# Log decays of each SSD head fetched from DRAM over all partitions instead of spread by TensorE, and the first four heads' exponentials one half earlier on ScalarE

## What is computed

```
acs = jnp.cumsum(dtc * a.reshape(g, r), axis=2)
acs_t = jnp.moveaxis(acs, 2, -1)
seg = acs_t[..., :, None] - acs_t[..., None, :]
decay_in = jnp.exp(jnp.where(lower, seg, -jnp.inf))
cb = jnp.einsum('bcign,bcjgn->bcgij', cc, bc)
xdt = xc * dtc[..., None]
y_diag = jnp.einsum('bcgij,bcgrij,bcjgrp->bcigrp', cb, decay_in, xdt)
```

## Time and profile before

| | us |
|---|---|
| median of 3 runs (2890.13 to 2893.3) | 2892.05 |
| the profiled execution | 2892.8 |
| its span, first to last instruction | 2890.1 |
| PE busy | 2823.3 (98%) |
| DVE busy | 1770.8 (61%) |
| ACT busy | 1498.3 (52%) |
| share of the DMA queue of SP (q1) in 16 engines | 55.5% |

### The profile page before, as it was taken

How to read it: one execution, slowest core, us unless ns; L and a number is a source line. 1 busy time by engine, 2 the same in 40 slices (tenths; PEclk the granted TensorE clock), 3 DMA queues, 4 the chain that set the end, 5 groups by cost and what they waited for, 6 DMA issues and landing times.

```text
span 2890.1 us, 41967 instructions
## 1 busy us (share of the span) xinstructions
PE 2823.3 (98%) x17088; PEld 2398.9 (83%) x17088; DVE 1770.8 (61%) x2255; ACT 1498.3 (52%) x2226; POOL 219.4 (8%) x275
## 2 busy tenths in 40 slices
PE   7999999999999999999989999999999999999997
PEld 4888998888777898877669889988887888897886
DVE  2487888886444555544455878888864444554555
ACT  3356776774333445533334567767743434544443
POOL 0001111120000000000110011111200000000000
PEclk9999999999999999999999999999999999999999
DMA  9944445545777644567896454455457565554664
GB/s 392 339 159 161 159 163 170 181 153 197 279 273 290 207 159 151 172 244 274 285 345 180 161 167 154 164 175 178 155 194 287 196 201 172 161 175 153 204 219 174
DMA packets 166849, 594.28 MB, mean 206 GB/s; under 512 B 20500, under 2 KB 22804, under 8 KB 166272
## 3 DMA queue, kind: packets, MB, share of 16 engines
q1 hardware_dynamic: 155376, 558.24, 55.5%
q0 software_dynamic: 11216, 33.34, 4.1%
q10 hardware_dynamic: 64, 0.02, 0.0%
HBM read 577.85 MB, written 13.66 MB: 205 GB/s over the span
## 4 chain that ended last, share of the span: by engine, by line
PE 86%; DMA 6%; DVE 5%; ACT 1%; issue 1%; SPq 0%; DVEq 0%; POOLq 0%; POOL 0%; ACTq 0%
PE PM L413 18%; PE PM L425 17%; PE PM L414 17%; PE PM L429 7%; PE PM L418 7%; PE PM L419 7%; PE A L638 5%; DMA raw<-in_w_in 2%; PE A L450 2%; DMA raw<-in_w_out 2%; DMA Zt<-in_w_mod 2%; DVE w_l L391 2%; PE A L635 1%; DVE X L1422 1%; DVE arena L1382 1%; PE PM L635 1%
## 5 line engine op out<-in xcount | busy, mean ns | idle before, releaser
L391 DVE TENSOR_TENSOR w_l<-raw,w_h 128x1024 fp32r<-128x1024 f32 (+1 forms) x880 | 1058.2, 1213 | 986.1 <-ACT w_h L386 977.3
L386 ACT ACTIVATE w_h<-raw 128x1024 fp32r<-128x1024 f32 (+1 forms) x880 | 905.4, 1046 | 827.5 <-PE PM L425 304.7
L413 PE MATMUL PM<-w_h,hT_h 128*128 128x512 f32 x1408 | 565.2, 401 | 2.1 <-issue 2.1
L414 PE MATMUL PM<-w_h,hT_l 128*128 128x512 f32 x1408 | 550.0, 391 | 0.0
L418 PE MATMUL PM<-hT_h,w_h 128*128 128x256 f32 x1920 | 485.6, 291 | 4.8 <-ACT w_h L386 2.5
L419 PE MATMUL PM<-hT_l,w_h 128*128 128x256 f32 x1920 | 469.7, 282 | 0.0
L413 PE MATMUL PM<-w_h,Z 128*128 128x512 f32 x1024 | 405.4, 396 | 9.5 <-ACT w_h L386 5.8
L414 PE MATMUL PM<-w_h,Z 128*128 128x512 f32 x1024 | 399.5, 390 | 0.0
L418 PEld LDWEIGHTS PM<-hT_h,w_h 128*128 128x128 f32 x1920 | 366.5, 191 | 16.2 <-issue 7.2
L425 PE MATMUL PM<-w_l,hT_h 128*128 128x512 f32 x1408 | 377.7, 390 | 0.7 <-DVE w_l L391 0.7
L419 PEld LDWEIGHTS PM<-hT_l,w_h 128*128 128x128 f32 x1920 | 367.1, 191 | 6.6 <-issue 4.8
(11 more groups left out here) (191 smaller groups left out, 2272.7 us busy)
## 6 DMA issues: line engine op xcount, KB each, us to landing
raw<-in_w_in SPq DMA_DIRECT2D x608, 512.0 KB, 4.2
raw<-in_w_ps SPq DMA_DIRECT2D x128, 512.0 KB, 5.3
raw<-in_w_mod SPq DMA_DIRECT2D x112, 512.0 KB, 4.3
Zt<-in_w_mod SPq DMA_DIRECT2D x80, 512.0 KB, 14.1
raw<-in_w_pa SPq DMA_DIRECT2D x64, 512.0 KB, 4.4
raw<-in_w_out SPq DMA_DIRECT2D x64, 512.0 KB, 6.0
arena<-in_state_ssm_fwd POOLq DMA_DIRECT2D x16, 256.0 KB, 3.8
arena<-in_state_ssm_bwd POOLq DMA_DIRECT2D x16, 256.0 KB, 3.7
```

The lines of the kernel that those rows point to most:

```text
L386: act.activation(w_h[:, k % RING, :, 0:n], half_raw(k, n), ACT.Copy).then_inc(hi_ready, 1)
L391: dve.tensor_tensor(w_l[:, k % RING, :, 0:n], half_raw(k, n), w_h[:, k % RING, :, 0:n].bitcast(F32), ALU.subtract).then_inc(lo_ready, 1)
L413: pe.matmul(tok_out(s), hi[:, kt, tk], wh, start=kt == 0, stop=False, skip_group_check=True)
L414: pe.matmul(tok_out(s), lo[:, kt, tk], wh, start=False, stop=False, skip_group_check=True)
```

## The change

The 64 x 512 table of log decays is written once per layer to a DRAM scratch tensor `h_dram`, by ACT's queue. SP then copies a head's row of 2 KB into all 128 partitions of `E[h % 4]` (256 KB), 128 times in all. ACT's `Relu` reads and writes `E` in place. PE's `decay` matmul, `sel` and `H` are gone, and the transposed running sums are computed in one copy of 64 rows instead of two. `exp` of heads 0 to 3 stands one half earlier (behind halves 1 to 4), that of heads 4 to 7 stands where it was (behind halves 6 to 9). `squares` writes its unused squares to `zs` instead of `E[0]`.

```diff
 LOAD_OF_HALF, LOAD_OF_TILE = raw_order()
+def decay_loads():
+    after = {}
+    for layer in range(DEPTH):
+        for q in range(NG):
+            body = 8 * layer * CHUNKS + 8 * (PH_SSD + 2 * (q + 1))
+            for h, at in enumerate((-1, 0, 5, 6, 11, 12, 13, 14)):
+                after[body + at] = (layer, q, h)
+    return after
+DECAY_LOADS = decay_loads()
 HOLDS = dict([(n, ("half", i)) for i, n in enumerate(LOAD_OF_HALF)] + [(n, ("tile", i)) for i, n in LOAD_OF_TILE.items()])
...
                 sp.dma_start(Zt[:, z_slot(m), :], mod_words(m)).then_inc(z_loaded[z_slot(m)], DMA)
+            def decay_row(L, q, h):
+                G = L * NG + q
+                if q == 0 and h == 0:
+                    sp.wait_ge(s_("H_stored"), (L + 1) * DMA)
+                if h >= 4:
+                    sp.wait_ge(s_("y_part"), G * HG + h - 3)
+                elif h >= 2:
+                    sp.wait_ge(s_("stT_done"), G + 1)
+                elif G:
+                    sp.wait_ge(s_("y_part"), (G - 1) * HG + 5 + h)
+                row = h_dram[L, q * HG + h:q * HG + h + 1, :].to_broadcast([P, 4 * P])
+                sp.dma_start(E[h % 4].rearrange("p d s n -> p (d s n)"), row).then_inc(e_loaded[h % 4], DMA)
             def half(L, c, i, w, block):
...
                     tile_to_z(m)
+                if k in DECAY_LOADS:
+                    decay_row(*DECAY_LOADS[k])
             def chunk(L, c, w, block, halves=8):
...
                     pe.wait_ge(s_("chw_ready"), L + 1)
-                    pe.wait_ge(s_("const_cast"), 1)
                     fp32(A[:, 3, 0:256].rearrange("p (d s n) -> p d s n", d=2, s=2)[:, 0], Umat, SA[:, 8:10, :], True)
...
                     for ds in range(4):
-                        for w in range(2):
-                            mm = fp32(A[NH * w:NH * w + NH, 0, ds * P:(ds + 1) * P], SA[:, 8 + ds, :], (Umat, Lmat)[ds // 2], ds == 0)
+                        mm = fp32(A[0:NH, 0, ds * P:(ds + 1) * P], SA[:, 8 + ds, :], (Umat, Lmat)[ds // 2], ds == 0)
                     mm.then_inc(s_("acsT_done"), 1)
...
                     mm.then_inc(s_("stT_done"), 1)
-                def decay(q, h):
-                    if h == 0:
-                        pe.wait_ge(s_("H_ready"), L + 1)
-                        pe.wait_ge(s_("ST_ready"), L * NG + q + 1)
-                    if h >= 2:
-                        pe.wait_ge(s_("exp_done"), (L * NG + q) * HG + h - 1)
-                    b = A[:, 2 + h % 2, :]
-                    mm = pe.matmul(b, sel[:, q * HG + h:q * HG + h + 1].to_broadcast([P, P]), H[:].rearrange("p d s n -> p (d s n)"),
-                                   start=True, stop=True, skip_group_check=True)
-                    mm.then_inc(s_("decay_done"), 1)
                 def y_start(q):
...
                     for h in range(HG):
-                        st[h] = [lambda h=h: decay(q, h)] + st.get(h, [])
                         st[4 + h] = st.get(4 + h, []) + [lambda h=h: y_diag(q, h)]
...
                         .then_inc(s_("conv_silu"), 1)
-                def H_hi():
+                def H_copy():
                     act.wait_ge(s_("acsT_done"), L + 1)
-                    act.activation(H[:].rearrange("p d s n -> p (d s n)"), A[:, 0, :], F.Copy).then_inc(s_("H_hi"), 1)
+                    act.activation(Hs[:], A[0:NH, 0, :], F.Copy).then_inc(s_("H_copied"), 1)
+                    act.wait_ge(s_("H_copied"), L + 1)
+                    act.dma_start(h_dram[L], Hs[:]).then_inc(s_("H_stored"), DMA)
                 def decays():
...
                       33: [lambda: bc_silu(0), lambda: center(1)], 36: [lambda: bc_silu(1), lambda: center(2)],
-                      38: [H_hi], 39: [lambda: bc_silu(2)]}
+                      38: [H_copy], 39: [lambda: bc_silu(2)]}
                 if L == 0:
...
                     xT_copy(3)
-                    act.wait_ge(s_("masks_loaded"), DMA)
-                    act.activation(sel[:], sel32, F.Copy).then_inc(s_("const_cast"), 1)
                     h_hi(0)
...
                     G = L * NG + q
-                    act.wait_ge(s_("decay_done"), G * HG + h + 1)
-                    if h >= 4:
-                        act.wait_ge(s_("y_part"), G * HG + h - 3)
+                    act.wait_ge(e_loaded[h % 4], (G * 2 + h // 4 + 1) * DMA)
                     e = E[h % 4]
...
                         for s in range(2):
-                            ins = act.activation(e[:, d, s, :], A[:, 2 + h % 2, (2 * d + s) * P:(2 * d + s + 1) * P],
-                                                 F.Relu, scale=-1.0, bias=SA[:, 2 * d + s, q * HG + h:q * HG + h + 1])
+                            ins = act.activation(e[:, d, s, :], e[:, d, s, :], F.Relu, scale=-1.0,
+                                                 bias=SA[:, 2 * d + s, q * HG + h:q * HG + h + 1])
                     ch.link(ins)
...
                             ch.wait()
-                        ch.link(act.activation(E[0].rearrange("p d s n -> p (d s n)"), y[:, s], F.Square, accum_out=ss[:, s:s + 1]))
+                        ch.link(act.activation(zs[:, s], y[:, s], F.Square, accum_out=ss[:, s:s + 1]))
                     ch.wait()
...
                     for h in range(HG):
-                        st[2 + h] = [lambda h=h: exp(q, h)] + st.get(2 + h, [])
+                        at = 1 + h + h // 4
+                        st[at] = [lambda h=h: exp(q, h)] + st.get(at, [])
                     if q:
...
                         .then_inc(s_("tail_ready"), 1)
-                def H_lo():
-                    dve.wait_ge(s_("H_hi"), L + 1)
-                    Hl = H[64:128].rearrange("p d s n -> p (d s n)")
-                    tt(Hl, A[64:128, 0, :], Hl.bitcast(F32), ALU.subtract).then_inc(s_("H_ready"), 1)
                 def decay_dt():
...
                       34: [lambda: conv_bc(1, 0)], 35: [lambda: conv_bc(1, 1)], 37: [lambda: conv_bc(2, 0)],
-                      38: [lambda: conv_bc(2, 1)], 39: [H_lo, cumulative]}
+                      38: [lambda: conv_bc(2, 1)], 39: [cumulative]}
                 if L == 0:
```

More of the change, by code:

```diff
@@ L237, in build @@
         x_dram = nc.dram_tensor("x_scratch", (2, TOK, D_MODEL), F32).ap()
+        h_dram = nc.dram_tensor("log_decay_scratch", (DEPTH, NH, 4 * P), F32).ap()
         gate_dram = nc.dram_tensor("gate_scratch", (2, D_MODEL), F32).ap()
@@ L310, in build @@
         fng = part(2048, 5376)
-        sel32 = part(NH, 4864)
         modg = part(512, 0).rearrange("p (t n) -> p t n", t=2)
@@ L317, in build @@
         one = cst[0:P, K_U + P - 1:K_U + P]
-        sel = sb("sel", [P, NH], F32R)
         cond = sb("cond", [P, KT, 32])
@@ L325, in build @@
         SA = sb("SA", [P, NQ, NH])
-        H = sb("H", [P, 2, 2, P], F32R)
+        Hs = sb("Hs", [NH, 4 * P])
         half_exp = sb("half_exp", [P, 2])
@@ L337, in build @@
         raw_loaded = [sem(f"raw_loaded{i}") for i in range(SLOTS)]
+        e_loaded = [sem(f"e_loaded{i}") for i in range(4)]
         z_loaded = [sem(f"z_loaded{i}") for i in range(Z_SLOTS)]
@@ L760, in cb @@
                         pe.wait_ge(s_("conv_silu"), L * 12 + 3)
-                        pe.wait_ge(s_("H_ready"), L + 1)
+                        pe.wait_ge(s_("H_copied"), L + 1)
                         pe.wait_ge(s_("tail_ready"), L + 1)
@@ L835, in final_states @@
                 def final_states(q):
-                    pe.wait_ge(s_("exp_done"), (L * NG + q) * HG + HG)
                     pe.wait_ge(s_("xw_ready"), L * NG + q + 1)
@@ L1871, in _ @@
                 pool.dma_start(x2[:, s], v).then_inc(s_("x_loaded"), DMA)
-            pool.dma_start(sel32, a["cst"][:, K_SEL:K_WIDTH]).then_inc(s_("masks_loaded"), DMA)
             wait_alone(pool, s_("half_exp_set"), 1)
```

## The result

| | before | after |
|---|---|---|
| median of 4 runs each, us | 2892.68 (2890.13 to 2899.28) | 3291.86 (3285.92 to 3292.81) |
| ratio, with its 95% interval | | 1.137 [1.1357, 1.1383] |
| the profiled execution; its span | 2892.8; 2890.1 | 3290.95; 3289.1 |

The change costs 399.2 us; 3295 was forecast. First the page of the changed kernel: busy time, the chain that ended last, and the granted clock in 40 slices, to be held against the earlier trace rows.

The account below looks back on a forecast made before the run. PE, busy 98% of the span, was taken to bound the kernel. 2892.8 + 368 (per body 24.8 of waits less 1.84 of work, 16 bodies) + 35 (clock) - 1 (transposed sums) = 3295 us; range 3195 to 3390, 78%.

Parts of the forecast that it names:

- the ring: Heads 4 to 7: exp, hi_half, lo_half, load, copy, next exp wait in turn; PE waits 24.8 us per body.
- the flight that is left: A copy's flight for heads 4 to 7, from the end of a lo_half to the start of an exp: 4.2 us.
- the table loads: On ACT, exp 0 and 1 around z_silu: three loads instead of one, lo_half 6 1.97 us late per body.
- the slow clock: PE's half 10, behind the last gap, runs slow and is not covered: 2.2 us per body, 35 in all.
- PE's saving: On PE, 128 decay matmuls go: 1.84 us per body, 29.4 us in all.
- What was to be free and was: Copies of heads 0 to 3, the copies' volume (5% of what is moved) and ACT's Relus reading SBUF: cost 0.
- PE's idle time: A sign: PE's idle time before a half's first matmul, released by ACT's w_h, sums to 350 to 400 us.
- The announced gaps: PE's waits before halves 7 to 10 of a body: 9.3, 5.5, 5.0 and 5.0 us.
- the faster rival: The rows are in time and only PE's work goes: 2862 us, chance 3%.
- The flight is mostly hidden: Milder rival: with no flight at all, 6.2 us per body, 99 for 16, 2991 us; 2991 to 3195 has 8%.

Follow-up runs that it names:

- e3: The changed kernel with the copies of heads 4 to 7 issued two loads sooner, behind loads 9 to 12 instead of 11 to 14: 2953.74 us.
- e4: The changed kernel without copies, except those of heads 0 to 3 of the first group (its decays are not the reference's): 2923.58 us.
- e6: e4 with exp of head 0 put back behind z_silu, so one table load per body instead of three: 2892.07 us.
- e2: The changed kernel with the copies of heads 4 to 7 issued one load sooner, behind loads 10 to 13 instead of 11 to 14: 2999.05 us.
- e1: The changed kernel with exp of head 0 put back behind z_silu, so one table load per body instead of three: 3262.92 us.
- e8: The changed kernel with 512-column matmuls that nobody reads in PE's gaps, 24 behind step 6 and 16 behind steps 7, 8 and 9: 3279.27 us.
- e9: e6 with DVE's M of heads 0 to 3 one half sooner: 2878.27 us.

## Why the prediction was right, step by step

The 399 us in the order of the experiments, each taken off the one before: the ring 338 (after to e3), the flight that is left 30 (e3 to e4), the table loads 31.5 (e4 to e6), which sums to 399.8, the difference to within 1 us. The ring's 338 holds what the slow clock costs, and in none of the three is PE's saving paid out.

- **The ring.** Its steps were forecast as 10.2, 8.2 and 8.2 us from one `exp` to the next, 26.6 together; the chain shows 10.75, 8.55 and 8.09, 27.4, 0.8 more. From `lo_half` 6's end (497.05 in DVE's timeline) to `exp` 4 it is 4.11 (4.2 forecast), with the copy in flight for 3.7 in the median. The step of 8 us follows from the place in SP's queue, as e2 shows, not from anything that the copy is in itself. The body was to be 56.46 + 23.0 + 2.2 = 81.7 and is 80.88.
- **The table loads.** From the start of `z_silu`'s place to the end of `lo_half` 6 it was 22.80 us and is 24.82, from 472.23: 2.02 late against 1.97 forecast, 32 us in all. The pairs measured 28.9 to 32.1, and e1 at 3262.9 met the sum without them, 3263.
- **What was to be free and was.** Copies of heads 0 to 3 and the 32 MB of volume: no wait names them. ACT's Relus cost 390 ns each, 370 before, which with ACT waiting cost nothing that shows. (The 32 MB are 5.6% of what the kernel moves, not 5.)
- **The clock, mis-sized, and mostly covered.** The clock did fall to 0.50 behind gaps, and inside the ring that was free, as forecast. Two things failed. "2.8 x 0.22/0.12, less 2.8, is 2.2 us" (it is 2.3) takes half 10 as slow from end to end, but the clock is at 0.53 and 0.62 up to 535 us and at 1.00 behind it, and 1.4 us are lost there. And "Half 10 is the first behind the last gap and is not covered" is wrong in good part: the chain of DVE and ACT behind `lo_half` 10 is as long as PE's, so that a fast half 10 takes 0.28 us off a body and not 1.4. By the stretches the clock costs 4.5 us, by e8's time 12.6, not 35. The Trainium skill, page "TensorE: Matmul & The Clock Gate", section "HAM oscillation — how this bites in real kernels", describes bursts between DMA waits that start slow each time. Three of the four bursts here do, the one behind the gap of 2.31 us doesn't; and in this kernel they lie under other waits and cost little.
- **Where errors cancel.** The clock's term is 22 to 30 us too large. Against that stand the steps of the ring, 0.8 us a body or 13 us too small, and the 8 us outside the bodies, which the sum lacked. That the sum ends 3 us from the time is luck; that it lies in the range isn't.
- **PE's idle time, forecast at 350 to 400 us, is 273** (151.4, 98.2 and 23.4). The waits were worked out for warm halves and then held against a trace with slow ones. The announced gaps 9.3, 5.5, 5.0, 5.0 are 6.74, 3.62, 2.31, 3.08. Of the missing 9 us 6.5 are in the last three, where slow matmuls fill 7.2 us and the steps are 0.7 longer. The 2.6 of the first gap have another cause: half 6 ran at full clock, 0.12 us from one matmul to the next. The working let PE be ready for half 7 at 481.2, ahead of the 482.1 at which `lo_half` 6 ends, though half 6 needs that `w_l`. PE came free at 498.81, 1.76 behind the end of `lo_half` 6. The body's length doesn't hang on it, since `hi_half` 7 sets the start of half 7.
- **PE's saving.** The 29.4 us taken off were never there to be had alone: e6 is the kernel before to 0.1%, and e9 regains 13.8 of them. In the changed kernel this costs the forecast nothing, since the ring sets the body and PE waits in it anyway. It does fell the reasoning of the faster rival. With rows in time the changed kernel stands at 2923.6 (e4), and without the added table loads at 2892 (e6), not at 2862.
- **"The flight is mostly hidden", priced at 2991,** isn't what the trace shows: the flight of each copy of heads 4 to 7 lies in the chain in full. That e2 comes to 2999 is no sign for it, as e2 moves the copies' place and doesn't shorten their flight.

## What to carry to other kernels

A transfer that feeds an engine costs what its place in the queue costs: find what the queue waits for just ahead of it, and if that wait ends only with work queued behind the transfer's reader, each transfer adds its whole flight: steps of 8 us where PE needed 3. Issued two loads sooner the same copies cost 30 us in place of 368. A function of another table moved past one step cost two table loads a body here, 1.8 to 2.0 us. Work taken from the bound engine was worth nothing until the next engine's order (here DVE's `M`) let it be, and a half that the clock slows costs only what it sticks out over the other engines' chain.

## What the runs showed of the hardware

- PE's granted clock was at 0.50 or near it behind gaps of 3.1, 3.6 and 6.7 us. Behind one of 2.3 it was at 1.00 for the first 1.1 us and then at 0.50. PE's busy time rose by 116 us with less work. Busy share is no measure of what PE is worth in a stalled kernel.
- A 2 KB row of DRAM copied over 128 partitions (256 KB), right behind a load of 512 KB, landed in 3.7 us in the median (3.0 to 6.3). The POOL copies of the earlier trace rows, 6.7 in the median, were no guide to it.
- One more such copy ahead of it in the queue cost 1.34 us: 0.9 until the useful one lands, the rest at SP's issue. The issue of a load of 512 KB took SP 0.33 us in the ring, that of a copy 0.43, in both kernels.
